# Attention of a hybrid decoder layer: value products of a batch issued in two halves, with one logits product between them

## The chip, the core and the metric

The kernel runs on one core of a Trainium2 chip. The metric is the time of one execution in microseconds (us) on that core. TensorE is called PE in the profile (its weight loads are PEld), VectorE is DVE, ScalarE is ACT, GpSimd is POOL and SyncE is SP.

## What is computed

One layer with two branches over 2048 positions and 16 meta tokens, width 1024. An input projection feeds an RWKV-7 branch and a stick-breaking attention branch; both are gated, projected, merged and added to the input. The change concerns the attention branch alone, which has 16 heads of 64 channels:

```python
logits = jnp.einsum("bhqd,bhkd->bhqk", q[:, :, qs:qe], k[:, :, :qe]) * scale
visible = jnp.arange(qe)[None, :] < jnp.arange(qs, qe)[:, None]
log_keep = jnp.where(visible, jax.nn.log_sigmoid(-logits), 0.0)
log_between = lax.cumsum(log_keep, axis=3, reverse=True) - log_keep
weights = jnp.where(visible, jnp.exp(jax.nn.log_sigmoid(logits) + log_between), 0.0)
outs.append(jnp.einsum("bhqk,bhkd->bhqd", weights, v[:, :, :qe]))
```

In the kernel the weights are never formed: a running product of the keep probabilities (`kept`) is multiplied with differences of neighbouring values (`dv`), which gives the same sum.

## The kernel before

Three phases follow each other: the projections (to about 2029 us of the profiled span), attention (to about 2954 us), and the RWKV chunks with the output projections (to the end).

Attention walks through 64 groups. A group is four query tiles of 128 of one head; its rank, 0 to 3, says how far down the sequence it lies, and the ranks run 0, 1, 2, 3, 3, 2, 1, 0 over two heads. In this text a group is named by its number modulo 8, so 0 to 7 are one period of two heads, and there are eight periods. Group 2 has rank 2, groups 3 and 4 rank 3.

Three kinds of work go through PE:

- A logits product (`logits`, lines 1194 and 1195): two matmuls of up to 512 key columns into one of ZB = 3 banks `z`. ACT turns it into `keep` (a sigmoid, line 1251, KB = 6 buffers), and DVE scans that into `kept` (lines 1286 and 1289).
- A turn (`turn`, line 1205): up to four transposes of `kept` for one key tile kt into one of TB = 3 banks `turned`, which ACT copies into one of 18 buffers `w` (line 1261). A group of rank r has 4r + 5 turns, kt = -1 to 4r + 3.
- A batch of value products (`values`, line 1232): for each turn of the batch one or two matmuls of 64 output channels. Even and odd key tiles write different halves of the bank `acc`, and two neighbouring steps are issued together so that they run side by side. Key tiles that lie in the group's own queries have an extra 128-column matmul with `dv_diag`. At the end of a group a "sum" adds the two halves (ACT line 1266, DVE lines 1295 and 1299), and SP stores `y`.

The waits that the steps below touch are these:

```python
# logits:  reach(pe, keep_done, num - ZB + 1)
# turn:    if kt < 0:
#              pe.wait_ge(scanned, last_logits[g] + 1)
#          reach(pe, copied, num - TB + 1)
# values:  pe.wait_ge(copied, steps[-1][1] + 1)
# ACT:     act.wait_ge(logits_done, num + 1)
#          reach(act, scanned, num - KB + 1)
```

So the first turn of a group waits until DVE has scanned that group's last logits, and a turn waits until ACT has copied the turn three before it.

All engines follow one list, which `attention_schedule` (line 924) writes out by hand. For each turn it calls `issue(wanted(turned + AHEAD_OF), 1)`, which puts at most one logits product behind the turn when the straight-line plan `wanted` asks for it. After a batch of turns (nine or eight, or fewer at a group's end) it appends the value products of the batch before (line 971), and then `issue(wanted(turned), len(logits))` makes up whatever logits are behind the plan. `issue` does nothing where the next logits would overwrite a `kept` buffer that is still being turned.

Of the kernel before, what the change touches and what calls it, by code (L numbers as in the profile page):

```python
# [890 lines left out]
def rank(g):  # L891


    turn = g % (2 * GROUPS)
    return min(turn, 2 * GROUPS - 1 - turn)
# [10 lines left out]
def kept_earlier(g):  # L906

    return next((e for e in range(g - 1, -1, -1) if kept_in(e) == kept_in(g)), None)


def logits_of(g):

    pieces = {qt: pieces_of(qt) for qt in range(GROUP * rank(g), GROUP * (rank(g) + 1))}
    deepest = max(len(x) for x in pieces.values())
    return [(qt, *x[i]) for i in range(deepest) for qt, x in pieces.items() if i < len(x)]


def batches_of(g):

    steps = list(range(-1, GROUP * (rank(g) + 1)))  # L920
    return [steps[0:BATCH + 1]] + [steps[at:at + BATCH] for at in range(BATCH + 1, len(steps), BATCH)]


def attention_schedule():

    logits = [(g, *row) for g in range(GROUPS_ALL) for row in logits_of(g)]
    upto = [sum(len(logits_of(e)) for e in range(g + 1)) for g in range(GROUPS_ALL)]
    begins = [sum(GROUP * (rank(e) + 1) + 1 for e in range(g)) for g in range(GROUPS_ALL + 1)]  # L930
    due = [(0, upto[0])]
    for g in range(1, GROUPS_ALL):
        due.append((max(begins[g] - LEAD, due[-1][0] + 1), upto[g]))

    def wanted(step):
        for (x0, y0), (x1, y1) in zip(due, due[1:]):
            if step <= x1:
                return y0 + (y1 - y0) * max(0, step - x0) / (x1 - x0)
        return len(logits)

    order, done, turned = [], 0, 0
    previous = {}

    def issue(count, most):
        nonlocal done
        for _ in range(most):
            if done >= min(count, len(logits)):
                return
            g, qt, k0, size = logits[done]
            if kept_earlier(g) is not None and turned < begins[kept_earlier(g) + 1]:  # L950
                return
            order.append(("logits", g, qt, k0, size, done, previous.get((g, qt))))
            previous[g, qt] = done
            done += 1

    issue(upto[0], upto[0])
    held, finished = [], []
    for g in range(GROUPS_ALL):
        for batch in batches_of(g):
            for kt in batch:  # L960
                issue(upto[g], upto[g])
                order.append(("turn", g, kt, turned))
                turned += 1
                if finished and turned >= finished[0][1]:
                    order.append(("sum", finished.pop(0)[0]))
                issue(wanted(turned + AHEAD_OF), 1)
            held.append((g, [(kt, begins[g] + kt + 1) for kt in batch]))
            if len(held) > 1:
                of, steps = held.pop(0)
                order += [("sum", e) for e, _ in finished]  # L970
                order.append(("values", of, steps))
                finished = [(of, turned + 4)] if steps[-1][0] == GROUP * (rank(of) + 1) - 1 else []
            issue(wanted(turned), len(logits))
    order.append(("values", *held.pop(0)))
    return order + [("sum", e) for e, _ in finished] + [("sum", GROUPS_ALL - 1)]
# [73 lines left out]
def attention_phase(nc, sem, t, io, scratch, a, head0, y_sent, load_chunk):  # L1049

    order = attention_schedule()
    ZB, TB = 3, 3
    last_logits = {e[1]: e[5] for e in order if e[0] == "logits"}
# [1312 lines left out]
```

## Time and profile before

| | us |
|---|---|
| median of 3 runs | 4181.73 |
| lowest, highest | 4177.43, 4183.73 |
| profiled execution | 4181.06 |
| its span, first to last instruction | 4179.3 |
| attention phase in it | about 2029 to 2954 |

The profile is of one execution. The profiled time is 1.8 us longer than its span. Matmuls are pipelined: the start of each is sound, the duration of each overlaps the next one, so costs on PE are read as the distance from one start to the next.

### The profile page before, as it was taken

Reading aid. Unit: us, or ns where it says so; the run is one execution under the profiler, and the core shown is the slowest. Engines: PE = TensorE matmul, PEld = TensorE weight load, DVE = VectorE, ACT = ScalarE, POOL = GpSimd, SP = SyncE. Lnnn points to the kernel's source line nnn. Section 1 sums busy time; section 2 is a strip of 40 time slices with the busy share of each in tenths; the row PEclk is TensorE's granted clock in tenths of the full one; section 3 lists DMA queues with packets and bytes.
Section 4 is the critical chain, followed back from the end, with each engine's and each line's share of the span. In section 5 each row is a group of like instructions: output and inputs, shape, how many; then the busy total and the mean of one; then the engine's idle time right before and its main releaser. Section 6 shows DMA issues by size and latency. Waiting matters only on the chain. (4 is left out here: it accounts for less than half of the span.)

```text
span 4179.3 us, 88867 instructions
## 1 busy us (share of the span) xinstructions
PE 4018.9 (96%) x34728; PEld 3324.1 (80%) x34728; DVE 2326.8 (56%) x3166; ACT 1708.9 (41%) x3428; POOL 816.5 (20%) x658
## 2 busy tenths in 40 slices
PE   7999999998899999999799999999899999899999
PEld 6888998887688888888666666666789888888887
DVE  5444545434643444444578888888567777633222
ACT  4222322222322222222367767776556655521111
POOL 3101111110311011111000000000256666600222
PEclk9999999999899999999899999999999999999999
DMA  2343332334233443433544344443333333375653
GB/s 90 116 124 116 109 107 96 105 120 147 67 110 115 121 121 114 120 100 116 132 93 87 84 97 100 96 101 76 92 112 109 104 107 113 82 219 165 207 177 126
DMA packets 482562, 479.67 MB, mean 115 GB/s; under 512 B 256784, under 2 KB 366992, under 8 KB 476128
## 3 DMA queue, kind: packets, MB, share of 16 engines
q1 hardware_dynamic: 469360, 445.85, 38.3%
q10 hardware_dynamic: 11520, 25.17, 1.7%
q0 software_dynamic: 1392, 4.54, 0.4%
q8 instruction: 212, 3.47, 0.3%
q14 instruction: 78, 0.64, 0.1%
HBM read 305.51 MB, written 169.93 MB: 114 GB/s over the span
## 5 line engine op out<-in xcount | busy, mean ns | idle before, releaser
L1251 ACT ACTIVATE keep<-z 128x512 f32<-128x512 f32 (+4 forms) x704 | 366.9, 532 | 182.6 <-PE z L1195 174.7
L1289 DVE TENSOR_TENSOR_SCAN kept<-keep,kept 128x512 f32<-128x512 f32 (+2 forms) x448 | 403.9, 951 | 22.5 <-ACT keep L1251 15.8
L1261 ACT COPY w<-turned 128x512 f32<-128x512 f32 (+4 forms) x704 | 367.3, 548 | 103.1 <-PE turned L1205 102.5
L1205 PE MATMUL turned<-t_identity,kept 128*128 128x128 f32 (+1 forms) x2432 | 372.8, 276 | 31.7 <-DVE kept L1289 17.0
L1205 PEld LDWEIGHTS turned<-t_identity,kept 128*128 128x128 f32 (+1 forms) x2432 | 280.7, 135 | 106.5 <-ACT w L1261 24.2
L1286 DVE TENSOR_TENSOR_SCAN kept<-keep,hidden 128x512 f32<-128x512 f32 (+3 forms) x256 | 274.9, 1113 | 153.3 <-ACT keep L1251 152.5
L1194 PE MATMUL z<-k_high,q_parts 128*128 128x512 f32 (+4 forms) x704 | 298.7, 425 | 19.4 <-DMA k_low<-scr_k_lo 12.6
L1232 PE MATMUL acc<-w,dv 128*64 128x512 f32 (+3 forms) x1280 | 289.7, 540 | 0.0
L1195 PE MATMUL z<-k_low,q_parts 128*128 128x512 f32 (+4 forms) x704 | 252.8, 360 | 0.0
L1767 POOL TENSOR_TENSOR off<-NT,tri 128x512 f32<-128x512 f32 x165 | 205.6, 1273 | 141.5 <-ACT NT L1661 141.5
L1232 PEld LDWEIGHTS acc<-w,dv 128*64 128x64 f32 x1280 | 94.7, 137 | 135.5 <-issue 116.5
L1582 PE MATMUL even<-T,off 64*64 64x64 f32 x5280 | 195.5, 222 | 5.0 <-issue 3.0
L1582 PEld LDWEIGHTS even<-T,off 64*64 64x64 f32 x5280 | 175.4, 136 | 20.0 <-issue 5.3
L1194 PEld LDWEIGHTS z<-k_high,q_parts 128*128 128x128 f32 x704 | 134.6, 191 | 53.5 <-issue 32.8
L1311 POOL DMA_DIRECT2D dv_diag<-scr_v_edge x15 | 7.3, 485 | 836.2 <-DMA dv_diag<-scr_dv 836.2
L1751 DVE STREAM_TRANSPOSE T<-T 128x256 f32<-128x256 f32 x264 | 117.6, 445 | 86.5 <-ACT T L1686 83.7
L1686 ACT COPY T<-odd 128x256 f32<-128x256 f32 x264 | 98.2, 372 | 160.3 <-PE odd L1595 148.3
L1741 DVE TENSOR_TENSOR X<-even,eye 128x256 f32<-128x256 f32 x330 | 139.3, 422 | 43.7 <-PE even L1582 36.0
L2108 DVE TENSOR_TENSOR y_lo<-y_raw,y_hi 128x512 fp32r<-128x512 f32 x61 | 45.3, 742 | 204.2 <-ACT y_hi L2052 204.2
L1595 PE MATMUL odd<-X,T 64*64 64x64 f32 x4224 | 151.6, 219 | 2.5 <-issue 2.2
L794 DVE CAST w_hi0B<-w_raw0B 128x1024 fp32r<-128x1024 f32 x40 | 41.6, 1041 | 197.2 <-PE pp3B L340 69.3
L794 DVE CAST w_hi0A<-w_raw0A 128x1024 fp32r<-128x1024 f32 x40 | 32.6, 814 | 203.0 <-PE pp4A L340 76.4
(566 smaller groups left out, 10884.5 us busy)
## 6 DMA issues: line engine op xcount, KB each, us to landing
w_raw0A<-in_w_main SPq DMA_DIRECT2D x42, 512.0 KB, 3.9
w_raw0B<-in_w_main SPq DMA_DIRECT2D x42, 512.0 KB, 3.9
w_raw1A<-in_w_main SPq DMA_DIRECT2D x41, 512.0 KB, 3.8
w_raw1B<-in_w_main SPq DMA_DIRECT2D x41, 512.0 KB, 3.9
KB<-scr_kb SPq DMA_DIRECT2D x33, 512.0 KB, 5.2
AR<-scr_ar SPq DMA_DIRECT2D x33, 512.0 KB, 6.0
y_raw<-scr_y SPq DMA_DIRECT2D x64, 256.0 KB, 4.5
merge<-scr_merge SPq DMA_DIRECT2D x64, 256.0 KB, 5.7
```

The lines of the kernel that those rows point to most:

```text
L1194: pe.matmul(out, queries, k_high[u][:, k0:k0 + size], start=True, stop=False)
L1195: pe.matmul(out, queries, k_low[u][:, k0:k0 + size], start=False, stop=True).then_inc(logits_done, 1)
L1205: mm = pe.transpose(turned[num % TB][0:size, P * r:P * r + P], kept[kept_in(g)][:, src:src + size], t["identity"][:, :])
L1232: mm = pe.matmul(out, lhs, rhs, start=start, stop=stop, skip_group_check=True)
L1251: act.activation(keep[num % KB][:, 0:size], z[num % ZB][:, 0:size], ACT.Sigmoid, scale=-DH ** -0.5).then_inc(keep_done, 1)
L1261: act.copy(w[num % WB][0:size, c0:512], turned[num % TB][0:size, c0:512]).then_inc(copied, 1)
L1286: dve.tensor_tensor_scan(dst, data, hidden[:, 512 - size:][:, ::-1], 1.0, ALU.mult, ALU.max).then_inc(scanned, 1)
L1289: dve.tensor_tensor_scan(dst, data, data, kept[kept_in(g)][:, end:end + 1], ALU.mult, ALU.bypass).then_inc(scanned, 1)
L1582: mm = pe.matmul(x_bank(half)[hs, k, :], off[lv - 1][hs, HP * half + k, :], T2[hs, half, 0, k, :], start=True, stop=True)
L1595: mm = pe.matmul(p_bank(half)[hs, 0, k, :], T2[hs, half, 1, k, :], X[hs, half, k, :], start=True, stop=True)
L1741: dve.tensor_tensor(X[:, half, :, :], x_bank(half), eye[:, :].unsqueeze(1).broadcast_to([P, HP, C]), ALU.add).then_inc(s["x_out"], 1)
L1767: pool.tensor_tensor(out, a, b, op).then_inc(s[name], 1)
```

## The change

```diff
             if len(held) > 1:
                 of, steps = held.pop(0)
                 order += [("sum", e) for e, _ in finished]
-                order.append(("values", of, steps))
+                order.append(("values", of, steps[:len(steps) // 2]))
+                issue(wanted(turned) + 1, 1)
+                order.append(("values", of, steps[len(steps) // 2:]))
                 finished = [(of, turned + 4)] if steps[-1][0] == GROUP * (rank(of) + 1) - 1 else []
             issue(wanted(turned), len(logits))
```

Each batch becomes two entries of the list. A batch of nine becomes four and five steps, eight becomes four and four, five becomes two and three, four becomes two and two. Between them `issue` may put one logits product. The very last batch is made in one piece as before. The operations, their shapes and their number stay the same; only the order of the list changes, on PE, ACT and DVE alike.

## Rows read from the trace of the kernel before

**Rows 1.** The page, busy time of the engine: us, share, instructions.
```profile
PE 4018.9 (96%) x34728; PEld 3324.1 (80%) x34728; DVE 2326.8 (56%) x3166; ACT 1708.9 (41%) x3428; POOL 816.5 (20%) x658
```

**Rows 2.** Windows: PE, PEld, DVE, ACT, POOL busy, clock, DMA; two periods of attention.
```profile
2188.25:2300.65 112.40, 108.70 (x704) 76.59 (x705) 93.92 (x106) 79.67 (x184) 0.97 (x2) 1.00 0.45 96
2300.65:2413.06 112.41, 108.78 (x704) 76.59 (x704) 93.87 (x105) 79.73 (x184) 0.97 (x2) 1.00 0.44 95
```

**Rows 3.** Waits in the attention phase: who waited for whom, us, times, longest.
```profile
PE turned L1205 <- DVE kept L1289: 17.0, 10, 2.1
PE turned L1205 <- ACT w L1261: 14.0, 17, 0.9
...
PE z L1194 <- DMA k_low<-scr_k_lo: 12.6, 1, 12.6
```

**Rows 4.** Timeline of PE around a batch of nine: start, duration, what.
```profile
2314.83 0.47 PE L1194 MATMUL z<-k_high,q_parts 128*128 128x512 f32 x1
...
2315.47 4.50 PE L1232 MATMUL acc<-w,dv 128*64 128x512 f32 x18
2319.90 0.50 PE L1194 MATMUL z<-k_high,q_parts 128*128 128x512 f32 x1
...
2320.47 0.39 PE L1194 MATMUL z<-k_high,q_parts 128*128 128x512 f32 x1
...
2320.93 0.60 PE L1205 MATMUL turned<-t_identity,kept 128*16 128x128 f32 x4
2321.28 0.48 PE L1194 MATMUL z<-k_high,q_parts 128*128 128x512 f32 x1
...
2321.84 0.60 PE L1205 MATMUL turned<-t_identity,kept 128*128 128x128 f32 x4
2322.19 0.48 PE L1194 MATMUL z<-k_high,q_parts 128*128 128x512 f32 x1
```

**Rows 5.** Timeline of PE's weight loads in the same batch.
```profile
2315.46 0.20 PEld L1232 LDWEIGHTS acc<-w,dv 128*64 128x64 f32 x4 [0.36 <-ACT w L1261]
2315.95 0.14 PEld L1232 LDWEIGHTS acc<-w,dv 128*64 128x64 f32 x2 [0.29 <-issue]
...
2318.52 0.14 PEld L1232 LDWEIGHTS acc<-w,dv 128*64 128x64 f32 x1 [0.29 <-issue]
```

**Rows 6.** Timeline of PE after group 2's second batch, and group 3's last turn.
```profile
2330.60 0.66 PE L1205 MATMUL turned<-t_identity,kept 128*128 128x128 f32 x4
2331.01 0.31 PE L1194 MATMUL z<-k_high,q_parts 128*128 128x144 f32 x1
...
2331.27 0.62 PE L1205 MATMUL turned<-t_identity,kept 128*128 128x128 f32 x4
...
2335.97 0.33 PE L1205 MATMUL turned<-t_identity,kept 128*128 128x128 f32 x1 [0.94 <-ACT w L1261]
```

**Rows 7.** Timeline of PE, two turns with no logits between them.
```profile
2267.41 1.03 PE L1205 MATMUL turned<-t_identity,kept 128*128 128x128 f32 x8
2268.20 0.26 PE L1194 MATMUL z<-k_high,q_parts 128*128 128x16 f32 x1
```

**Rows 8.** Timeline of PE before the first turn of a group 2.
```profile
2298.38 0.39 PE L1194 MATMUL z<-k_high,q_parts 128*128 128x512 f32 x1
...
2300.65 0.60 PE L1205 MATMUL turned<-t_identity,kept 128*16 128x128 f32 x4 [1.65 <-DVE kept L1289]
```

**Rows 9.** Timeline of DVE in the 18 us before that turn.
```profile
2282.66 2.59 DVE L1289 TENSOR_TENSOR_SCAN kept<-keep,kept 128x400 f32<-128x400 f32 x3 [0.23 <-ACT keep L1251]
2285.16 0.66 DVE L1295 TENSOR_TENSOR total<-acc,low_half 64x512 f32<-64x512 f32 x1
...
2296.95 3.65 DVE L1289 TENSOR_TENSOR_SCAN kept<-keep,kept 128x144 f32<-128x144 f32 x5
```

**Rows 10.** Timeline of ACT before group 3's last turn.
```profile
2334.24 0.58 ACT L1266 COPY low_half<-acc 64x512 f32<-64x512 f32 x1
2334.85 0.60 ACT L1251 ACTIVATE keep<-z 128x512 f32<-128x512 f32 x1
```

## The prediction

> **What bounds the kernel now.** I read the page first: PE is busy 96% of the span [rows 1]. Then the windows of attention, where the change lies. Two whole periods take 112.4 us each, with PE busy for 108.7, the clock at its full 1.00 (2.4 GHz), DVE busy for 93.9 and ACT for 79.7 [rows 2]. PE sets the pace; only 3.7 us of a period are idle on it, so the most that a better order could ever give back is that. Third, the waits of the phase, to see what these 3.7 us are: turns that wait for a scan of DVE (17.0 us in 10 waits), turns that wait for a copy of ACT (14.0 us in 17), and one load of head 1's keys (12.6 us) [rows 3]. All other time is matmuls one behind the other, so the question is what a matmul costs beside which neighbour. The timeline of PE answers that, from start to start.
>
> **What the change does to the list.** I worked through the schedule function with its rules. Of 96 batches 95 are cut. In 62 a logits product lands between the halves; in the others `issue` has nothing to give (both batches of group 5, the second ones of groups 3 and 4, and the last group 6's), and the halves stand side by side. Such a pair costs nothing: same matmuls in the same order, the pairs of neighbouring steps stay whole (all first halves have an even number of steps), and the second half's wait is for copies made several turns before. No logits, turn or value product is added. In the 62, the inserted product is the one that followed the batch before, or, in the second batch of group 2, one that stood between two turns.
>
> **Price of one cut on PE.** Three terms, each from a place where PE changes between full-width and half-width matmuls.
>
> 1. Opening and closing a run of value products. A batch of nine takes 2319.90 - 2315.47 = 4.43 us [rows 4]. Inside it the weight loads advance by (2318.52 - 2315.95)/6 = 0.428 us, and a pair of steps takes two such advances, 0.857 [rows 5]. Four pairs and the lone ninth step need 5 x 0.857 = 4.285. The remaining 0.145 is paid once for each run; part of it shows in the first advance, 2315.95 - 2315.46 = 0.49 in place of 0.43 [rows 5]. Two runs in place of one: +0.145.
> 2. A logits product behind value products takes 2320.47 - 2319.90 = 0.57, one behind another logits product 2320.93 - 2320.47 = 0.46 [rows 4]. The cut adds one more such start: +0.11.
> 3. A logits product ahead of value products takes 2315.47 - 2314.83 = 0.64; between two turns it takes 2321.84 - 2321.28 = 0.56 [rows 4]. One more such entry: +0.08.
>
> Together 0.335 us where the product comes out of the run of two or three that made up the backlog behind a batch (groups 0, 1, 3, 4, 7, and the first batch of 2). In group 6 one logits product follows the batch and then a turn; the turn now stands behind value products, which costs 2331.01 - 2330.60 = 0.41 against 2322.19 - 2321.84 = 0.35 [rows 6, 4]: 0.145 + 0.08 + 0.06 = 0.285. In the second batch of group 2 the product leaves a place between turns. It took 2331.27 - 2331.01 = 0.26 there [rows 6] and takes 0.26 - 0.08 + 0.11 + 0.08 = 0.37 between the halves. Behind it two turns now touch: (2268.20 - 2267.41) - 0.35 = 0.44 for the first of them in place of 0.35 [rows 7, 4], +0.09. That makes 0.145 + 0.37 - 0.26 + 0.09 = 0.345. The same group's last turn waits 0.94 us for ACT [rows 6]. There one keep of 512 columns, 0.60 us on ACT [rows 10], moves out of ACT's queue, but the logits that made it, 0.55, also leave PE's; the wait stays within 0.1. I take 0.35.
>
> Here the Trainium skill speaks against the change: TensorEngine Tiling, section Tiling Modes, says that changing the tiling mode drains the engine. It gives no price; TensorE: Matmul & The Clock Gate, Part 2, puts a drain at about 128 cycles. At 2.4 GHz two drains for each cut would be an estimated 0.11 us, so 4.9 us for the 46 cuts counted below. The rows hold three times that, and the sum goes by the rows.
>
> **What hides some of it.** The first turn of group 2 waits 1.65 us for DVE [rows 8]. DVE runs without a gap from 2282.66, its last idle time (0.23 us, waiting for a keep) [rows 9], through two sums and 16 scans, until group 2's last scan ends at 2300.6. The batches of groups 7 and 0 lie within this chain. Their two cuts delay PE by 0.67, but PE would come to that turn at 2298.38 + 0.46 = 2298.84 and now comes at 2299.5, still more than a microsecond early. So 15 cuts (7 of group 7, 8 of group 0) cost nothing; this cover is good for 1.65 us and is used to 0.67. The chain starts with a scan of logits made behind group 6's batch, and these come 0.285 later, so group 6's cut is paid in full. The cut of the first group 1 lies ahead of the 12.6 us wait for keys [rows 3], whose loads hang on a sum before it: hidden too. That leaves 31 x 0.335 = 10.4, 8 x 0.35 = 2.8 and 7 x 0.285 = 2.0: 46 cuts, 15.2 us.
>
> **What it gives back.** The logits in the middle let ACT and DVE start about 2 us earlier on one product. Their gaps close by that, but outside the chain above nobody on PE waits for them: DVE is busy for 94 of 112 us [rows 2]. In the chain DVE's start is set by a logits product that is not moved ahead, so its end does not come earlier. I take 0. The bounds: nothing, or all waits of turns, 31.0 us [rows 3].
>
> **Sum.** 4181.06 + 15.2 = 4196.3 us against the profiled execution. This stands 0.7 below the median shown, so I say 4196.5, 0.35% slower. From no change a measurement of this kernel tells about 0.2%, 8.4 us.
>
> **Rivals.**
>
> - A: the cover fails. DVE's chain starts later by more than PE does, or PE's path to group 2 is longer than it looks, and the 16 hidden cuts are paid: 16 x 0.335 = 5.4 more, 4202. For it: ACT's and PE's rings are full in that stretch, so small stalls can add. Against it: 1.65 us of slack. 0.13.
> - B: no difference. The opening and closing belong to the batch's shape, not to the break, and the logits in the middle hide their own start because the next weights load ahead. Then only the entry, 0.08, is paid: 46 x 0.08 = 3.7, 4185. Against it: both ends of each batch show their gap, wherever it stands. The estimate from the Trainium skill's drain (TensorE: Matmul & The Clock Gate, Part 2), 4186, would land here. 0.09.
> - C: faster. The earlier logits shorten the waits of turns for DVE and ACT. If all 31.0 us go, nothing is hidden either, and the cuts cost 15.2 + 5.4 = 20.6: 4181.06 - 31.0 + 20.6 = 4170.7. It decides from two thirds of these waits on. Against it: the waits for ACT come where a sum's copy (0.58) and a full keep (0.60) stand ahead of the copy that is waited for [rows 10], and these stay in the queue; and DVE's chain is full. 0.04.
> - D: the list hardly changes. Excluded by the count: 62 insertions.
>
> The forecast has 0.74. A and the forecast are slower, B is the same, C is faster: faster 0.04, same 0.09, slower 0.87. The range: from 4189 (term 1 measures 0 for the 46 cuts, 6.7 less) to 4203 (A); C, B and the rest beyond hold under 2 in 10.
>
> **What the profile of the changed kernel would show.** The period of about 112.4 us grows to about 114.3, the clock stays at 1.00, PE's idle time falls by 0.3 to 0.4 in each. The batch of nine splits into runs of 8 and 10 matmuls of about 1.86 and 2.72 us, with a logits product of about 0.66 between. The wait at group 2's first turn falls from 1.65 to about 1.3, since PE comes 0.67 later and DVE's chain 0.285 later. The wait for ACT at the end of groups 3 and 4 stays at 0.85 to 1. The first period's wait for keys shrinks by a third of a microsecond and ends at the same 2087. I am wrong if the two runs add up to 4.43 (B), if a period grows by 2.6 (A), or if a period is shorter than 112.4 (C).

## Result: 0.33% slower, as forecast

The changed kernel takes 4192.3 us (median of 8 runs, 4190.7 to 4195.4) against 4180.3 for the one before (8 runs, 4173.8 to 4183.7). The ratio is 1.0033, with a 95% interval of 1.0024 to 1.0042: 10 to 18 us more. The forecast was 15.2 us more, 4196.5, in a range of 4189 to 4203.

Whole times of one kernel spread by some 10 us. In the profiles of the eleven kernels of this document, the time outside the attention phase, which no edit touches, lies between 3250.0 and 3259.3 us. Inside the phase the periods repeat to some hundredths of a microsecond (one of the six whole periods before takes 112.62, the others 112.34 to 112.41), so the experiments are read from the phase, from its first to its last matmul. Each kernel has one profile, and the part of the phase ahead of the first whole period moves by more than that with the granted clock, as will be seen; it is kept apart where it matters. The view by windows of the profile before gives the phase as its window (same columns as in [rows 2]):

```profile
2029.14:2954.39 925.25, 879.46 (x5632) 617.52 (x5632) 749.87 (x830) 639.19 (x1471) 8.63 (x19) 0.98 0.41 89
```

The same view after the change, with the phase and two whole periods, which answer to [rows 2]:

```profile
2026.63:2965.50 938.87, 899.98 (x5632) 609.38 (x5632) 751.99 (x830) 644.08 (x1471) 8.62 (x19) 0.99 0.41 88
...
2185.54:2299.90 114.36, 111.52 (x704) 75.55 (x705) 94.11 (x105) 80.30 (x184) 0.97 (x2) 1.00 0.44 94
2299.90:2414.36 114.46, 111.62 (x705) 75.57 (x705) 94.10 (x105) 80.33 (x184) 0.97 (x2) 1.00 0.43 93
```

The phase grew by 938.87 - 925.25 = 13.6 us. A period grew from 112.41 to 114.46, by 2.05 (2.01 as the mean of the six whole periods). PE's work is the same 704 matmuls of a period, yet it is busy 2.8 us longer, and its idle time fell from 3.7 to 2.8. The timeline of PE around the batch that [rows 4] show, now in two runs:

```profile
2314.41 0.47 PE L1196 MATMUL z<-k_high,q_parts 128*128 128x512 f32 x1
...
2315.04 1.94 PE L1234 MATMUL acc<-w,dv 128*64 128x512 f32 x8
2316.91 0.51 PE L1196 MATMUL z<-k_high,q_parts 128*128 128x512 f32 x1
...
2317.58 2.79 PE L1234 MATMUL acc<-w,dv 128*64 128x512 f32 x10
2320.30 0.51 PE L1196 MATMUL z<-k_high,q_parts 128*128 128x512 f32 x1
...
2320.87 0.60 PE L1207 MATMUL turned<-t_identity,kept 128*16 128x128 f32 x4
2321.23 0.48 PE L1196 MATMUL z<-k_high,q_parts 128*128 128x512 f32 x1
```

From start to start the runs take 1.87 and 2.72 us, 4.59 together where the whole batch took 4.43, and the logits product between them takes 0.67. From the product ahead of the batch to the first turn it is 2320.87 - 2314.41 = 6.46 us; in [rows 4] the same work took 2320.93 - 2314.83 = 6.10. That is 0.36 for one insertion.

The starts of the groups' first turns tell where in a period the 2.05 us lie. In the period from 2300.65 before and from 2299.90 after, the turns of group 2 take 0.69 us more (20.97 against 20.28), those of group 3 0.75, of group 4 0.36 and of group 7 0.25. Those of groups 5 and 6 don't change, and the 0.35 more of group 0 comes back at the end of group 1's, in the wait at group 2's first turn. The value products of a batch are issued a batch of turns later, so these four are, in this order, the cuts of group 1 and of group 2's first batch; of group 2's second and group 3's first; of group 4's first; and of group 6.

The first turn of group 2, timeline of PE, answers to [rows 8], and the last turn of group 3 to [rows 6]:

```profile
2298.32 0.40 PE L1196 MATMUL z<-k_high,q_parts 128*128 128x512 f32 x1
...
2299.90 0.60 PE L1207 MATMUL turned<-t_identity,kept 128*16 128x128 f32 x4 [0.95 <-DVE kept L1291]
...
2336.32 0.33 PE L1207 MATMUL turned<-t_identity,kept 128*128 128x128 f32 x1 [0.85 <-ACT w L1263]
```

The wait for DVE fell from 1.65 to 0.95: this is where the cuts of groups 7 and 0 hide. The wait for ACT stayed, 0.85 in place of 0.94. In the view of waits, after the change, against [rows 3]:

```profile
PE turned L1207 <- ACT w L1263: 13.1, 16, 0.9
...
PE z L1196 <- DMA k_low<-scr_k_lo: 11.8, 1, 11.8
...
PE turned L1207 <- DVE kept L1291: 11.8, 10, 2.1
```

### The profile page after: what moved, and what is told of

It reads as the page before. It is cut to its first block and busy times, and to the rows that moved or that the text cites. A ratio compares the mean times of both kernels' runs of the same rounds, so it can differ in the third digit from the quotient of the medians.

```text
span 4188.9 us, 88867 instructions
## 1 busy us (share of the span) xinstructions
PE 4038.5 (96%) x34728; PEld 3315.8 (79%) x34728; DVE 2328.7 (56%) x3166; ACT 1713.9 (41%) x3428; POOL 816.6 (19%) x658
## 3 DMA queue, kind: packets, MB, share of 16 engines
q10 hardware_dynamic: 11520, 25.17, 1.7%
## 5 line engine op out<-in xcount | busy, mean ns | idle before, releaser
L1196 PE MATMUL z<-k_high,q_parts 128*128 128x512 f32 (+4 forms) x704 | 304.1, 432 | 18.6 <-DMA k_low<-scr_k_lo 11.8
L1234 PE MATMUL acc<-w,dv 128*64 128x512 f32 (+3 forms) x1280 | 300.4, 542 | 0.0
```

Of the source, the lines that this page charges most:

```text
L1196: pe.matmul(out, queries, k_high[u][:, k0:k0 + size], start=True, stop=False)
L1234: mm = pe.matmul(out, lhs, rhs, start=start, stop=stop, skip_group_check=True)
```

## Experiments

All start from the kernel before and are compared with it. The first four take the change apart.

**The cut alone.** The halves are issued without the logits between them.

```diff
-                order.append(("values", of, steps))
+                parts = [0] + ([len(steps) // 2] if True else []) + [len(steps)]
+                for k in range(len(parts) - 1):
+                    order.append(("values", of, steps[parts[k]:parts[k + 1]]))
```

> Every batch is issued as two halves, with nothing between them. Theory (PE pays for changing between full-width and half-width matmuls, 0.335 us at each insertion of a logits product): no difference, within 3 us of before; a batch of nine keeps its 4.43 us. Rival (the cut itself costs, through the second half's own wait and a broken run): 0.145 us at each of 95 cuts, 14 us slower, much like the change.

Measured: ratio 1.0002 (0.9993 to 1.0011). Windows of the phase and one period, and the batch of nine in the timeline of PE:

```profile
2026.50:2951.30 924.80, 879.03 (x5632) 617.20 (x5632) 749.96 (x830) 639.15 (x1471) 8.66 (x19) 0.98 0.42 89
2297.64:2410.02 112.38, 108.73 (x705) 76.57 (x705) 93.90 (x105) 79.71 (x184) 0.97 (x2) 1.00 0.45 94
...
2312.44 4.50 PE L1234 MATMUL acc<-w,dv 128*64 128x512 f32 x18
2316.88 0.51 PE L1196 MATMUL z<-k_high,q_parts 128*128 128x512 f32 x1
```

The period is the old one, and the batch takes 4.44 us. Ninety-five cuts and as many extra waits cost nothing; the rival, 14 us, is out. What costs is what stands in the cut.

**Only the cuts of groups 7 and 0, and all cuts but these.**

```diff
-                order.append(("values", of, steps))
+                parts = [0] + ([len(steps) // 2] if of % 8 in (7, 0) else []) + [len(steps)]
+                for k in range(len(parts) - 1):
+                    order.append(("values", of, steps[parts[k]:parts[k + 1]]))
+                    if k + 2 < len(parts):
+                        issue(wanted(turned) + k + 1, 1)
```

The second kernel has `not in` for `in`.

> Only the batches of groups 7 and 0 are cut, each with one logits product between the halves: 15 insertions, all within DVE's unbroken chain ahead of group 2's first turn. Theory (PE's wait for DVE there covers them): within 3 us of before, and that wait falls by about 0.67 us from 1.65. Rival A (the cover fails): 15 x 0.335 = 5 us slower.

> All batches but those of groups 7 and 0 are cut: 47 insertions, 46 of them open. Theory: the same time as the change itself, 13 to 15 us over before, since the 15 left out cost nothing; the wait at group 2's first turn rises above before's 1.65 to about 1.9, as DVE's chain starts 0.285 later. Rival A: 47/62 of the change's cost, about 10 us.

Measured: ratio 0.9998 (0.9989 to 1.0007) for the 15 cuts of groups 7 and 0, and 1.0039 (1.0026 to 1.0053) for the other 47. The period of the first, and PE's wait at group 2's first turn in it:

```profile
2295.83:2408.22 112.39, 109.46 (x704) 76.17 (x705) 93.88 (x105) 79.87 (x184) 0.97 (x2) 1.00 0.44 94
...
2295.83 0.60 PE L1209 MATMUL turned<-t_identity,kept 128*16 128x128 f32 x4 [0.94 <-DVE kept L1293]
```

Phase and period of the second:

```profile
2024.70:2963.70 939.00, 894.88 (x5632) 612.36 (x5632) 751.97 (x830) 642.91 (x1471) 8.65 (x19) 0.99 0.41 88
2298.13:2412.58 114.45, 110.91 (x704) 75.97 (x704) 94.10 (x105) 80.16 (x184) 0.97 (x2) 1.00 0.44 93
```

The two cuts in DVE's chain make PE 0.73 us busier in each period (109.46 against 108.73 with the bare cut), take 0.71 from its wait, and leave the period at 112.39. The other cuts give the full 114.45; the two phases, 939.0 here and 938.9 with the change, are the same. The cover holds, and rival A is out. The expectation that the wait would rise to 1.9 in the second kernel was wrong: the waits of turns for DVE are 17.0 us in 10 there, as before. Group 6's cut delays PE and DVE's chain alike, so it can't change the wait between them.

**A logits product behind every pair of steps.**

```diff
-                order.append(("values", of, steps))
+                parts = [0] + ([at for at in (2, 4, 6) if at < len(steps) - 1] if True else []) + [len(steps)]
+                for k in range(len(parts) - 1):
+                    order.append(("values", of, steps[parts[k]:parts[k + 1]]))
+                    if k + 2 < len(parts):
+                        issue(wanted(turned) + k + 1, 1)
```

> Batches are cut behind every pair of steps (at 2, 4 and 6), with up to one logits product in each gap: 180 insertions in place of 62. Theory: (180 - 16) x 0.335 = 55 us over before, about 4235. Rival (what costs is the moving of logits ahead of the plan, or one delay for each batch, not the number of breaks): the cost stays near the change's 12 to 15 us.

Measured: 4231.1 us, ratio 1.0117 (1.0102 to 1.0133), some 49 us more. Phase and period:

```profile
2027.20:3000.50 973.30, 937.37 (x5632) 593.79 (x5632) 759.73 (x830) 657.20 (x1471) 8.66 (x19) 0.99 0.39 85
2309.06:2427.80 118.74, 116.55 (x705) 73.80 (x705) 95.09 (x105) 82.11 (x186) 0.97 (x2) 1.00 0.42 89
```

Timeline of PE at the first turn of a group 2, and in a batch of nine of this kernel:

```profile
2309.06 0.60 PE L1209 MATMUL turned<-t_identity,kept 128*16 128x128 f32 x4 [0.16 <-DVE kept L1293]
...
2324.81 1.08 PE L1236 MATMUL acc<-w,dv 128*64 128x512 f32 x4
2325.82 0.51 PE L1198 MATMUL z<-k_high,q_parts 128*128 128x512 f32 x1
...
2326.48 1.08 PE L1236 MATMUL acc<-w,dv 128*64 128x512 f32 x4
2327.49 0.51 PE L1198 MATMUL z<-k_high,q_parts 128*128 128x512 f32 x1
...
2328.16 1.08 PE L1236 MATMUL acc<-w,dv 128*64 128x512 f32 x4
```

Each pair takes 1.01 us where 0.857 of it is work, 0.15 more, every time; each logits product takes 0.67. The cost grows with the number of insertions, not with the number of batches, and the rival (12 to 15 us) is out. A whole period has 23 of the insertions, 7.7 us at 0.335 each, and it grew by 6.3 (118.74 against 112.41). The wait at group 2's first turn tells where the rest went: it fell from 1.65 to 0.16, so 1.49 us were covered, and 7.7 - 1.49 = 6.2. The expectation of 55 us took only the cuts of groups 7 and 0 as covered, 0.67 us a period; the cover held for more than twice that and was nearly used up. The insertions next ahead of it are group 6's three. That most of their cost was covered too, because the logits that start DVE's chain no longer stand behind the whole of group 6's batch, is argued, not shown apart.

The next two aim at the waits of turns, on which rival C rests.

**Sums one turn behind the batch**, `finished = [(of, turned + 1)]` in place of `turned + 4`.

> The kernel before with a group's sum placed one turn behind its last batch, not four. Theory (the ACT waits at the last turns of groups 3 and 4, 0.85 us in 15 places, come from the sum's copy of 0.58 us standing in ACT's queue there): each falls by 0.3 to 0.58, 4 to 9 us faster. Rival (ACT's queue is full there anyway, and the copy only moves ahead in it): within 2 us of before.

Measured: ratio 0.9997 (0.9988 to 1.0006). PE's waits for ACT fell from 14.0 us to 10.1, its waits for DVE from 17.0 to 14.9, yet the period rose to 112.74:

```profile
2294.60:2407.34 112.74, 109.91 (x704) 76.54 (x705) 93.57 (x105) 79.88 (x184) 0.97 (x2) 1.00 0.44 94
```

The waits for ACT now come in 26 small pieces, and PE's busy time went up by 1.1 (from 108.8) although nothing was added to it. Part of it can be seen in the timelines of PE, at the same place of the period. In the kernel before:

```profile
2396.34 0.27 PE L1205 MATMUL turned<-t_identity,kept 128*128 128x128 f32 x1
2396.36 0.48 PE L1194 MATMUL z<-k_high,q_parts 128*128 128x512 f32 x1
```

and with the early sums:

```profile
2390.55 0.27 PE L1205 MATMUL turned<-t_identity,kept 128*128 128x128 f32 x1
2390.89 0.50 PE L1194 MATMUL z<-k_high,q_parts 128*128 128x512 f32 x1
```

The same logits product starts 0.34 us behind the last transpose, not 0.02, and the row shows no idle time: most of the stall lies inside the modelled duration (0.27) of the matmul before it and counts as busy. The period is 0.3 us longer, so the rival is right. The phase is 923.8 us all the same, 1.5 shorter than before: head 1's keys are loaded behind the first group's sum, which now comes earlier, and the wait for them fell from 12.6 to 10.3. The whole time doesn't tell these apart.

**Logits asked for one turn earlier**, `LEAD` 4 in place of 3.

> The kernel before with the plan asking for each group's logits one turn earlier (LEAD 4 in place of 3). Theory (group 2's first turn waits 1.8 us for DVE's chain, whose start is set by when PE makes the logits behind group 6's batch): DVE starts the chain earlier, the wait shrinks by up to 1.8 in 7 places, up to 12 us faster. Rival (group 2's logits may not start sooner, as their buffer is still being turned; more turns stand side by side and wait for ACT's copies): within 4 us, or slower by up to 5.

Measured: 4186.4 us, ratio 1.0013 (1.0003 to 1.0022). The waits in the view of this kernel, and a period:

```profile
PE turned L1205 <- ACT w L1261: 25.0, 32, 1.0
...
PE turned L1205 <- DVE kept L1289: 4.8, 10, 2.1
...
2300.01:2412.75 112.74, 109.48 (x704) 76.26 (x705) 93.55 (x105) 80.26 (x185) 0.97 (x2) 1.00 0.44 93
```

The wait for DVE did fall, from 17.0 to 4.8 us, and ACT took most of it back, 14.0 to 25.0. One plan serves three engines, and a turn that no longer waits for a scan waits for a copy. The idle time that was won, 0.4 us a period, is more than lost in busy time (109.48 against 108.78). These waits don't account for the whole slowdown: the phase is 929.7 us, 4.4 longer, while the one wait for head 1's keys grew from 12.6 to 16.6. The rival (slower by up to 5) is nearest.

**Head 1's loads at the start of the phase.** Queries, keys and steps of head 1 are issued by SP ahead of its loop; before, they stood behind the first group's sum.

```diff
             load_gate(0)
             load_gate(1)
+            load_queries(1, qk_in[1])
+            load_keys(1, k_high, "k_hi", qk_in[1])
+            load_keys(1, k_low, "k_lo", qk_in[1])
+            load_steps(1, v_in[1])
```

`due_after(0)` is then empty.

> The kernel before with head 1's queries, keys and steps loaded by SP at the start of the attention phase and not behind the first group's sum. Theory: the 12.6 us wait for keys goes, and with it the half clock that follows it (17.1 us at 0.5, worth some 3 us), 12 to 17 us faster. Rival (the loads now collide with the first head's use of memory, or their issue delays the first gate and y transfers): 5 to 10 us faster.

Measured: 4161.4 us, ratio 0.9958 (0.9944 to 0.9971). The phase, and a period:

```profile
2025.70:2932.90 907.20, 873.67 (x5632) 614.75 (x5632) 749.59 (x830) 638.61 (x1471) 8.64 (x19) 1.00 0.42 91
2279.24:2391.57 112.33, 108.69 (x704) 76.57 (x704) 93.88 (x105) 79.70 (x184) 0.97 (x2) 1.00 0.43 94
```

The phase is 18.0 us shorter and the period hardly differs: all of it comes from the phase's first 160 us. The wait itself is 12.6. Behind it PE worked at half the clock for 6.4 us in the profile before, which costs half of that, 3.2. The last 2.2 are the granted clock too, but hang on no wait for keys: another stretch of 3.4 us at half the clock, 1.7, behind the first turn of the first group 2, which this profile hasn't and the next kernel's has although it loads early too; and a half-clock stretch at the phase's very start that ended 1.8 us sooner, 0.5. The first two sum to what the timelines show: the turns of the first group 2 took 25.17 us before, the wait left out, and take 20.25 here. The theory (12 to 17 us) covers the 15.8 that belong to the wait, and the rival (5 to 10) is out. This version beats both kernels.

**Early loads and early sums together.**

> Both edits: head 1's loads at the start of the phase and each sum one turn behind its batch. Theory: the gains add, 16 to 26 us faster than before. Rival for the sum: no more than the early keys give alone.

Measured: 4169.5 us, ratio 0.9971 (0.9959 to 0.9983). The phase:

```profile
2026.70:2939.40 912.70, 884.85 (x5632) 616.26 (x5632) 747.51 (x830) 640.41 (x1471) 8.62 (x19) 0.99 0.42 90
```

The phase is 5.5 us longer than with the early loads alone (912.7 against 907.2). About 2.1 of it is the clock of the first 60 us: this profile has the two stretches just named at half the clock. The other 3.4 go with the sums, which cost 0.4 us in each period here as by themselves. The gains don't add: 12 us (7 to 17) by the whole times, where the theory had 16 to 26.

**The change on top of the early loads.** This asks where the forecast's missing 1.6 us went.

> The change together with head 1's loads at the start of the attention phase, to be set against those early loads alone (profiled attention phase 907.24 us). Theory (the change costs 15.2 us and got some 1.6 back in the first period, by a shorter stretch at half clock behind the wait for keys): with that wait gone nothing is given back, and the first group 1's cut is open too, so the phase is 15.3 to 15.8 us longer than with the early loads alone. Rival (the 1.6 us belong to the cuts themselves): 13.4 to 14.0 us longer.

Measured: 4182.1 us, ratio 1.0010 (1.0001 to 1.0019). The phase:

```profile
2026.40:2950.20 923.80, 896.64 (x5632) 607.51 (x5632) 751.77 (x830) 643.55 (x1471) 8.60 (x19) 0.99 0.42 89
2284.55:2398.99 114.44, 111.60 (x704) 75.55 (x704) 94.12 (x105) 80.32 (x184) 0.97 (x2) 1.00 0.43 92
```

It is 923.8 - 907.2 = 16.6 us longer than with the early loads alone, a little above the 15.3 to 15.8 of the theory and well off the rival's 13.4 to 14.0. Half a microsecond of it can't be the cuts: the first group 1's first turn, ahead of every value product, comes 16.55 us into the phase here and 16.07 with the early loads alone, as the half clock at its start ended later (9.6 us into the phase, and 7.8). So 47 cuts that nothing hides cost 16.1 us, where the terms give 15.2 + 0.335 = 15.5. With the wait for keys gone, nothing is given back.

## Why the prediction was right

**Price of an insertion.** Predicted 0.145 + 0.11 + 0.08. Measured in the changed batch: 0.16 for the second run (4.59 against 4.43), 0.67 for the logits product between against the 0.46 that it took in a row of logits products, 0.21; together 0.37, or 0.36 by the whole stretch. The bare cut shows that without the full-width matmul between, none of it is paid. The weight loads show one thing more, in the batch before:

```profile
2319.90 0.19 PEld L1194 LDWEIGHTS z<-k_high,q_parts 128*128 128x128 f32 x1 [0.81 <-issue]
2320.01 0.19 PEld L1195 LDWEIGHTS z<-k_low,q_parts 128*128 128x128 f32 x1
2320.24 0.19 PEld L1194 LDWEIGHTS z<-k_high,q_parts 128*128 128x128 f32 x1
```

The weights of the first full-width matmul behind the run load only when that matmul starts, at 2319.90, and those of the `k_low` matmul load 0.23 us ahead of it (it starts at 2320.24). Whether the price is a drain of the engine, the weight load that doesn't run ahead, or both, no run separates. TensorEngine Tiling, section Tiling Modes, of the Trainium skill says that a change of tiling mode drains the engine. The trace agrees in kind: 0.36 us with a full-width matmul between, nothing without. Two drains of about 128 cycles each (the Trainium skill, TensorE: Matmul & The Clock Gate, Part 2) would be an estimated 0.11 us, three times too low here.

**Which cuts are open.** 46 of 62 by the forecast. The 15 of groups 7 and 0 were shown to cost nothing by themselves, and the 47 others to cost all of the change. The first group 1's cut shows in the wait for keys: PE came to it 45.61 us into the phase, 0.35 later than before (45.26), and the wait is shorter, 11.8 us against 12.6. The other 0.45 of it is that the keys themselves were there earlier.

**Per period.** The terms give 4 x 0.335 + 0.345 + 0.285 = 1.97; measured 2.05. Stretch by stretch, in the forecast's terms: group 2's turns 0.67, measured 0.69; group 3's 0.68, measured 0.75; group 4's 0.335, measured 0.36; group 7's 0.285, measured 0.25. So the terms hold one by one, and not only in their sum; the most that is off is 0.07 where group 2's second batch is cut.

**Sum.** 15.2 us against 13.6 in the phase (by the medians 12.1, in an interval of 10 to 18, which holds the spread outside the phase too): the large term that was missing is the clock in the first period. Windows from the first matmul behind the wait for keys to the first turn of group 3, in the profile before:

```profile
2086.99:2096.19 9.20, 9.20 (x24) 3.19 (x25) 1.22 (x1) 0.86 (x2) 0.49 (x1) 0.65 0.49 105
```

and the same work after the change:

```profile
2084.03:2092.09 8.06, 8.06 (x25) 2.71 (x26) 2.45 (x2) 1.19 (x2) 0.49 (x1) 0.79 0.65 124
```

Behind the 12 us in which PE stood still the granted clock was at 0.5, the lower of its two levels (1.2 GHz). It stayed there for 6.4 us of PE's work in the profile before and for 3.4 after (mean 0.65 and 0.79 of these stretches). So a stretch with one insertion more took 1.14 us less, 1.5 less than forecast. Two smaller terms nearly cancel: the wait for keys ended 0.45 us earlier in the phase than before, and all that follows the stretch grew by 15.2 where 45 cuts at the forecast's prices give 14.9. That makes 1.5 + 0.45 - 0.3 = 1.6.

The shorter half clock needs no cut. In the eight kernels that have the wait for keys, PE's work at half clock behind it lasts from 3.2 to 6.4 us. With the bare cut it is 6.3 (phase 924.8), with only the hidden cuts 3.3 (phase 923.4), and with the plan of LEAD 4, which cuts nothing, 3.2. So this part of the measured time is luck, whichever way it falls: had the clock risen as late as in the profile before, the phase would have grown by about 15.1 us.

**What was wrong in detail.** The wait at group 2's first turn was said to fall to about 1.3; it fell to 0.95. The text took 0.67 off for groups 7 and 0 and then added the chain's 0.285, but PE's arrival is late by the same 0.285. The sum didn't use that number. PE's idle time of a period fell by 0.8 to 0.9, not by 0.3 to 0.4, for the same reason and because the wait for ACT shrank by a tenth. The wait for keys shrank by 0.8, not by a third of a microsecond, and ended at 2084.0, not at 2087; 2.5 of these 3 us only say that the phase began earlier in this profile (2026.63 against 2029.14).

**The rivals.** A (cover fails) was excluded by the split kernels. B (only the entry, 0.08, is paid) is out by the batch itself: the two runs take 4.59 us and not 4.43, and the product between them 0.67. D (the list hardly changes) is out by the 62 insertions. C (faster by shorter waits): the waits of turns fell from 31.0 to 24.9 us, and 5.2 of the 6.1 are the cover being used. The early sums and the earlier plan show that these waits can be moved, but that they come back as others or as stalls within PE's busy time.

## What to carry to other kernels

Where PE is the bound, list what each kind of matmul costs beside each neighbour, from start to start, before the order is changed: runs of half-width matmuls have a price at each end (here about a third of a microsecond for each interruption), and ACT and DVE may stand without new logits for the 4.4 us of a batch while nobody waits for them: feeding them earlier gave nothing back here. Then look for the waits that do stop PE and ask which cuts lie ahead of them. A delay there was free up to nearly the wait's length (0.7 and 1.5 us of 1.65), if it doesn't also delay the work that is waited for, as group 6's cut did. The largest gain had nothing to do with the order: one load issued too late, 12.6 us of wait and the half clock behind it.

## What the runs showed of the hardware

- Full-width and half-width matmuls next to each other (4-byte inputs, clock at 1.00): a run of value products pays 0.145 us once, a logits product behind one takes 0.11 and ahead of one 0.08 more than beside its like. An insertion measured 0.36 in the changed batch. Cutting the list without putting anything between costs nothing (period 112.38 against 112.41).
- A wait of 12 us on PE was followed by a granted clock of 0.5, for 3.2 to 6.4 us of work in different kernels. With that wait gone the phase's length fell by 18.0 us, of which 15.8 are the wait and the half clock behind it.
- Stalls of a few tenths of a microsecond do not show as PE's idle time: with the early sums a logits product started 0.34 us behind a transpose and not 0.02, with no idle time in the row, and PE's busy time of a period rose by 1.1 with unchanged work.
